# A mixer block on one core: the shift matrices of the row maxima made by ScalarE instead of GpSimd

## The reference

```python
sc = einsum('bqgrd,bngd->bqgrn', qb, kc) * scale          # 63 compressed keys
pc = softmax(where(cval, sc, NEG));  o_c = einsum('bqgrn,bngd->bqgrd', pc, vc)
ss_ = einsum('bqgrd,bqgkd->bqgrk', qb, ksel) * scale      # selected blocks
ps = softmax(where(smask, ss_, NEG));  o_s = einsum(..., ps, vsel)
sw = einsum('bqgrd,bkgd->bqgrk', qb, kwb) * scale         # window of 512 keys
pw = softmax(where(wmask, sw, NEG));  o_w = einsum(..., pw, vwb)
o = gt[..., 0:1] * o_c + gt[..., 1:2] * o_s + gt[..., 2:3] * o_w
```

## Time and profile before

| | before |
|---|---|
| median of 3 runs | 1952.54 us (1951.99 to 1953.63) |
| profiled execution | 1953.54 us, its span 1951.8 us |
| TensorE busy | 1917.9 us, 98% of the span |
| VectorE busy | 1225.4 us, 63% |
| ScalarE busy | 843.1 us, 43% |
| GpSimd busy | 475.6 us, 24% |
| granted clock of TensorE | 0.997 in the mean, 1.00 throughout attention |

### The profile page before, as it was taken

How to read it: one execution, slowest core, us unless ns; L and a number is a source line. 1 busy time by engine, 2 the same in 40 slices (tenths; PEclk the granted TensorE clock), 3 DMA queues, 4 the chain that set the end, 5 groups by cost and what they waited for, 6 DMA issues and landing times.

```text
span 1951.8 us, 24937 instructions
## 1 busy us (share of the span) xinstructions
PE 1917.9 (98%) x9163; PEld 1566.5 (80%) x9163; DVE 1225.4 (63%) x1993; ACT 843.1 (43%) x1468; POOL 475.6 (24%) x379
## 2 busy tenths in 40 slices
PE   7999999999999999999999999999999999999999
PEld 7997666667888888888888888887888888888887
DVE  6858788987633553334683536449666666568974
ACT  4535688886433333332131223334343443444442
POOL 2002234322222332220000000004343534424620
PEclk9999999999999999999999999999999999999999
DMA  6300000011333123336512213312233323257342
GB/s 176 61 1 1 1 1 1 2 44 33 117 107 112 49 82 108 108 108 226 173 38 84 84 54 119 140 29 89 93 98 97 116 95 108 97 198 255 108 140 86
DMA packets 176485, 177.68 MB, mean 91 GB/s; under 512 B 25883, under 2 KB 135661, under 8 KB 176365
## 3 DMA queue, kind: packets, MB, share of 16 engines
q1 hardware_dynamic: 174797, 175.71, 28.5%
q10 hardware_dynamic: 1568, 0.39, 0.1%
HBM read 132.82 MB, written 43.25 MB: 90 GB/s over the span
## 4 chain that ended last, share of the span: by engine, by line
PE 89%; DVE 8%; ACT 1%; issue 1%; DMA 0%; POOL 0%; SPq 0%; DVEq 0%; ACTq 0%; POOLq 0%
PE bank L2788 14%; PE bank L2789 14%; PE bank L2790 14%; PE bank L2930 4%; PE bank L2932 4%; PE bank L2931 4%; PE bank L3044 4%; PE bank L3107 4%; PE bank L3103 4%; PE bank L3105 4%; PE bank L2672 2%; PE bank L2750 2%; PE bank L2781 1%; PE bank L2783 1%; PE bank L2782 1%
## 5 line engine op out<-in xcount | busy, mean ns | idle before, releaser
L2788 PE MATMUL bank<-t_h,block_h 128*128 128x512 f32 x320 | 125.9, 394 | 5.3 <-DVE t_l L2131 4.8
L2048 DVE TENSOR_TENSOR pair_l<-raw,pair_h 128x512 fp32r<-128x512 f32 x68 | 59.3, 873 | 109.5 <-ACT pair_h L1405 109.5
L2048 DVE TENSOR_TENSOR block_l<-raw,block_h 128x512 fp32r<-128x512 f32 x68 | 67.1, 991 | 95.3 <-ACT block_h L1405 95.3
L2789 PE MATMUL bank<-t_l,block_h 128*128 128x512 f32 x320 | 125.5, 392 | 0.0
L2790 PE MATMUL bank<-t_h,block_l 128*128 128x512 f32 x320 | 125.4, 392 | 0.0
L2788 PE MATMUL bank<-d_h,pair_h 128*128 128x512 f32 x320 | 124.5, 389 | 0.0
L2789 PE MATMUL bank<-d_l,pair_h 128*128 128x512 f32 x320 | 124.5, 389 | 0.0
L2790 PE MATMUL bank<-d_h,pair_l 128*128 128x512 f32 x320 | 124.5, 389 | 0.0
L3103 PE MATMUL bank<-right_h,left_h 128*128 128x512 f32 x308 | 119.8, 389 | 0.0
L3105 PE MATMUL bank<-right_l,left_h 128*128 128x512 f32 x308 | 119.8, 389 | 0.0
L3107 PE MATMUL bank<-right_h,left_l 128*128 128x512 f32 x308 | 119.8, 389 | 0.0
(11 more groups left out here) (418 smaller groups left out, 5242.2 us busy)
## 6 DMA issues: line engine op xcount, KB each, us to landing
raw<-in_w_in SPq DMA_DIRECT2D x60, 512.0 KB, 4.9
raw<-in_w_up SPq DMA_DIRECT2D x44, 512.0 KB, 5.0
left_raw<-spilled SPq DMA_DIRECT2D x77, 256.0 KB, 2.7
gates_kept<-kept SPq DMA_DIRECT2D x32, 512.0 KB, 2.6
spilled<-spill_s SPq DMA_DIRECT2D x44, 256.0 KB, 2.0
sig_all<-gates_kept SPq DMA_DIRECT2D x20, 512.0 KB, 3.3
raw<-in_w_branch SPq DMA_DIRECT2D x16, 512.0 KB, 4.0
block<-in_w_down SPq DMA_DIRECT2D x6, 1024.0 KB, 6.9
```

The costliest lines, as they stand in the source:

```text
L2048: nc.vector.tensor_tensor(operand_l(n), pair_source(n), operand_h(n).bitcast(F32), ALU.subtract).then_inc(pair_low, 1)
L2788: nc.tensor.matmul(out, wh, b[0][:, kt, :], start=start and kt == 0, stop=False, skip_group_check=seeded)
L2789: nc.tensor.matmul(out, wh, b[1][:, kt, :], start=False, stop=False, skip_group_check=seeded)
```

## The change

The multiplication on GpSimd goes. ScalarE makes the same matrices, one head at a time: four copies of the 128x128 identity, each scaled by one column of `nmx`. The waits are the same ones, now on ScalarE's queue. The sets of a slot are made at the head of the next slot on ScalarE, ahead of that slot's exponential; the first set comes before the loop. ScalarE's loop runs to the last slot, so all 48 are made.

```diff
-                nc.gpsimd.tensor_tensor(shift[:, n % SHIFTS, :, :], ident[:, :].unsqueeze(1).broadcast_to([P, REP, P]),
-                                        nmx[:, n % MAXIMA, 0, :].unsqueeze(2).broadcast_to([P, REP, P]),
-                                        ALU.mult).then_inc(shift_done, 1)
...
             pool.wait_ge(proj_done, NTILES)
-            make_shift(0)
             for slot in slots:
-                for n in slot["shifts"]:
-                    make_shift(n)
...
             projected(LAST)
+            def make_shift(n):
+                act.wait_ge(max_done, piece_end[n])
+                if tasks[n][3] > HALF:
+                    act.wait_ge(both_done, both_at[n] + 1)
+                if n >= SHIFTS:
+                    read = row_at[n - SHIFTS] if n % 3 < 2 else unit_at[last_unit[n - SHIFTS]]
+                    act.wait_ge(s_done, read + 1)
+                for r in range(REP):
+                    ins = nc.scalar.activation(shift[:, n % SHIFTS, r, :], ident[:, :], ACT.Copy,
+                                               scale=nmx[:, n % MAXIMA, 0, r:r + 1])
+                ins.then_inc(shift_done, 1)
+
+            make_shift(0)
             row_heads(0)
             shift_row(0)
...
+            before = ()
             for slot in slots:
+                for n in before:
+                    make_shift(n)
+                before = slot["shifts"]
```

## The result

The changed kernel takes 1979.72 us (median of 4 runs, 1978.94 to 1982.3); the kernel before, on the same chip, 1952.26 us (4 runs, 1951.9 to 1953.63). The ratio is 1.0139, its 95% interval 1.0126 to 1.0152: slower by 27.5 us. Its profiled execution took 1980.06 us, with a span of 1977.9. The forecast was 1978 us.

A forecast was written before the change was run, and what follows sets the result against it. Attention's middle was taken as nearly ScalarE-bound, though TensorE led the whole program's chain. 20.3 + 5.5 = 25.8 us on the profiled 1953.5 gave 1979.3; the runs' median being 1.0 lower, 1978 us, range 1961 to 1994.

The forecast's parts named there:

- What bounds the stage: In attention, ScalarE nearly fills the middle stretches, idle only 3.1 of 29.1 and 3.9 of 37.1 us.
- The price of a set: Four scaled copies on ScalarE take 0.29 us each, 1.16 us a set, bounds 0.80 and 1.54.
- The first set: Before the first row copy, ScalarE's existing waits hide 1.1 of this set's 1.16 us.
- GpSimd's silence at 0: In attention, GpSimd's dropped multiplications return about 8 us of VectorE time but shorten the program by 0.
- Waits for the maxima at 0: At the heads of slots, ScalarE's sets wait for a late maximum at one of 39 places; cost taken as 0.
- The excess, 20.3 us: Over attention's six stretches, set time exceeding ScalarE's idle: 0, 1.8, 4.4, 10.5, 2.1 and 1.5 us.
- The fifth of what is hidden, 5.5 us: In attention's last five stretches, a fifth of the 27.3 us of sets fitting ScalarE's idle is lost anyway.
- The sign that exponentials would no longer wait for scores: Expected mark in the changed kernel's attention profile: exponentials stop waiting for scores, and scores wait for exponentials; no size given.
- Hidden: Rival: in attention, copies cost 0.80 us a set and VectorE's 8 us come back, 1953 to 1961 us; chance 0.06.
- faster: Rival: in attention, VectorE's subtraction is the real wait and the stage shortens by 8 us, 1945 us; chance 0.02.
- Nothing hidden: Rival: all 48 sets in attention cost their full time, 55.7 us, 2008 us; chance 0.05.
- Held at the head: Rival: ScalarE waits for maxima at most of 39 slot heads as VectorE slips behind, 25 us more, 2003; chance 0.09.

The follow-up runs named there:

- the scaled spare copies: Kernel before, GpSimd still making the matrices, plus four unread scaled quarter-identity copies (32 partitions each) on ScalarE at each of 47 places: 2009.01 us.
- the doubled sets: Changed kernel with four unread scaled copies of a quarter of the identity added on ScalarE behind each of 47 sets: 2065.68 us.
- eight sets on ScalarE: Kernel before with only the matrices of tasks 0 to 7, in attention's first stretch, made on ScalarE, the other 40 on GpSimd: 1951.99 us.
- the run with tasks 33 to 47: Kernel before with only the fifteen sets of tasks 33 to 47, in attention's last two stretches, made on ScalarE, the others on GpSimd: 1963.46 us.
- the half copies: Kernel before, GpSimd still making the matrices, plus two unread scaled 128x64 copies on ScalarE at each of the sets' 47 places: 1960.02 us.
- the first experiments: Kernel before, GpSimd still making the matrices, plus four unread 32-partition copies per place on ScalarE: 2009.01 us scaled, 1988.9 us without the scale.

## Why the prediction was right

The time, the sign and the place were right, and so was the mechanism: a set costs what ScalarE has no reachable idle for. One term of the sum was mis-sized by more than half, and that the total still came within 2 us is in part luck. The steps, one by one:

**What bounds the stage.** Right. ScalarE had little idle in the middle stretches, and those lost 7.3 and 9.1 us. The first had 20 us, and lost nothing.

**The price of a set.** Forecast 0.29 us a copy, 385 ns long, 1.16 a set; measured 388 ns, 0.29 apart, 1.16 to 1.17 a set. The sum of a plain copy and what a column scale added to a wider one held. The ends of the range, 0.80 and 1.54, came from the same rows and weren't needed. The Trainium skill (ScalarE: Activation LUTs, What ACT_TABLE_LOAD costs) gives 186 ns plus 0.833 ns per column for such an instruction, 93 ns more for a scale that is read per partition, and 93 ns of overlap between neighbours. From these figures I estimate 386 ns at 128 columns and 332 at 64. The trace agrees for the real copies (388) and for the half ones (334); for the spare quarters of 32 partitions (396) the overlap is missing.

**The first set** hid, as said: attention began no later.

**GpSimd's silence at 0.** Right, and within 1.2 us shown by the run that keeps GpSimd busy. Over the stage VectorE got back 148 x 40 ns = 5.9 us (forecast 8), and had nothing to use them for: it waits 34.8 us for ScalarE. By the rule of the Trainium skill (SBUF — State Buffer, Who interferes with whom) a VectorE instruction with two SBUF inputs and a GpSimd instruction that reads SBUF exclude each other for a whole instruction. The longest single subtraction before, 1517 ns against a median of 684, allows that, since it is longer by less than one multiplication of 1312 ns. The 62.5 us that the rule could have meant in all were not there. The forecast "nearer 684" came out half way, at 726 in the mean.

**Waits for the maxima at 0.** Right, 1.8 us. The run one slot earlier shows that this was no matter of course: 25.8 us there.

**The excess, 20.3 us.** Close, by a count that was a little off. The order gives 6, 7, 6, 12, 8 and 8 sets by slots, but a set at the head of the slot with which a stretch begins runs ahead of that stretch's first exponential, and falls into the stretch before. By time there are 7, 7, 7, 11, 7 and 8. With these the same rule gives 0, 1.8, 5.5, 9.4, 0.9 and 1.5, 19.1 us. This explains most of why the third stretch lost more than forecast and the fourth less.

**The fifth of what is hidden, 5.5 us.** This is the term that was mis-sized: the idle that a set can't reach is 12.6 us. In the last five stretches 40 sets were to need 47.6 us, of which 20.3 had no idle to hide in, and 21.8 of the other 27.3 were to be hidden. Measured: 40 x 1.17 = 46.8 us of sets, and growth of 28.3. So 18.5 us were hidden. Of these, 14.8 are idle that was used, from 31.0 down to 16.2. The other 3.7 I had not counted: ScalarE's records show 43.1 us more busy time, not 46.8, as if more instructions overlapped their forerunner now that there is less waiting (the exponential is 586 and not 593 ns in the mean); how the 3.7 us divide is not shown. The idle that stayed, 16.2 us less 0.03 for each of 121 units, is 12.6 us unused, where I had allowed 5.5. It stayed because a late exponential makes scores late, and ScalarE then waits for those; the timeline at 284 to 292 us shows both waits. The sign that exponentials would no longer wait for scores failed for this reason: they still wait 19.6 us. One premise of the estimate doesn't follow from its rows. ScalarE was to have 0.3 to 0.5 us to spare per slot, but idle divided by units is 0.30, 0.20, 0.25, 0.30 and 0.23 us in the last five stretches. At that rate a set of 1.17 us needs four to six units to be made good, and a new set comes every 1.5 to 5 units. The mistakes partly cancel: 19.1 + 12.6 - 3.7 = 28.0, where these five stretches grew by 28.3 and the forecast had 25.8.

**The rivals.** "Hidden" and "faster" fell with the price and with VectorE's idle. (The 5.4 of 50.9 us named there are the idle of tiles 2 to 4 alone; tiles 5 to 7 have 9.6 of 66.1.) "Nothing hidden" (2008) fell with the free first stretch. "Held at the head" needs the sets a slot earlier.

**Left open.** No run changed the clock alone, so its share is an estimate from four pairs of tiles, 0.5 to 1.6 us for 3.4 us at the lower clock. In the changed kernel that makes about 1 us; for the scaled spare copies it would be 7 to 23 of the 55 us, and for the doubled sets 14 to 45 of 112, which the table of ScalarE's time per set doesn't separate. No version beat the kernel before: eight sets on ScalarE are level with it.

## What to carry to other kernels

Price work that moves to another engine against that engine's idle, stretch by stretch, and not against its busy share of the whole: ScalarE at 43% of the program had 4 of 37 us left where the work came thickest. Allow for idle that can't be reached, here nearly half of what looked free (12.6 of 27.4 us), and count operations by when they run, not by which loop turn lists them. In a queue in fixed order a wait is free only while its data leads; one slot of delay was worth 28 us here, the clock's share included.

## What was not expected of the hardware

The more ScalarE holds up TensorE, the more of attention TensorE spends at its lower clock. With ScalarE's sets on GpSimd (0), and at 1.17, 1.27, 1.61 and 2.8 us the time at 1.2 GHz within attention is 0, 3.4, 20.5, 48 and 96 us. The matmuls then start 0.43 us apart in place of 0.23, so an engine that was only waiting falls behind by itself. At the four places in four kernels that I looked at, the fall came after TensorE had stood idle: busy 1.10, 1.12, 1.58 and 2.10 of the 3.00 us ahead or just before. But not every fall comes from the sets, and not every idle time brings one. In the run with tasks 33 to 47 TensorE waits 2.35 us for a maximum at 181 to 183 us, long before any set is on ScalarE, and the clock is low from 184 us for 3.4 us. In the kernel before it waits 2.36 us at the same place, busy 0.80 of 3.00 us in both, and the clock stays at 1.00. The 3.4 us of the half copies lie at this place too (184 to 188 us). Each figure here is of one profiled execution.

ScalarE's copies of 32 partitions by 128, each at another partition offset of the same tile, don't overlap (396 ns, 0.40 apart; without the scale 305 ns, 0.32 apart), while those of 128x128 and 128x64 do, by 0.1 us. Whether the offset, the partition count or the shared tile decides was not tried. A substitute of the same length on paper was thus 0.44 us longer per set than the real one, and the first experiments with it missed.
